# Rotary angles between projections, and modulation loads ahead of most of x, in a two-block transformer kernel

## What is computed

```python
mod = jax.nn.silu(c) @ w_ada[l] + b_ada[l]
shift1, scale1, gate1, shift2, scale2, gate2 = jnp.split(mod, N_MOD, axis=-1)
h = modulate(rmsnorm(x, norm1_w[l]), shift1, scale1)
proj = h @ w_in[l]
r_q, r_k, r_v, r_g, d_q, d_k, d_v, d_z, d_a, d_b = jnp.split(proj, cuts, axis=-1)
rq = rotary(heads(r_q, RET_HEADS), positions)
rk = rotary(heads(r_k, RET_HEADS), positions)
ret = retention(rq, rk, heads(r_v, RET_HEADS))
...
def rotary(x, positions):
    ang = positions.astype(jnp.float32)[..., None] * inv_freq
    cos, sin = jnp.cos(ang)[:, :, None, :], jnp.sin(ang)[:, :, None, :]
```

## Time and profile before

| | |
|---|---|
| median of 3 runs | 3334.73 us (3334.26 to 3335.98) |
| the profiled execution | 3336.45 us |
| its span | 3334.6 us |
| TensorE busy | 3054.4 us (92%), 11914 matmuls |
| VectorE, ScalarE, GpSimd busy | 929.2, 622.1, 477.9 us |
| first TensorE instruction | 43.79 us |
| first projection | 57.69 us |
| mean granted clock of TensorE | 0.961 |

### The profile page before, as it was taken

One profiled execution on the slowest core, in us unless ns is written; L12 is line 12 of the kernel. 1 busy time (PEld: TensorE's weight loads), 2 busy tenths in 40 slices (PEclk: granted clock), 3 DMA queues, 4 the chain that ended last, 5 costly groups with the idle time before them and its releaser, 6 DMA issues.

```text
span 3334.6 us, 30020 instructions
## 1 busy us (share of the span) xinstructions
PE 3054.4 (92%) x11914; PEld 1712.6 (51%) x11914; DVE 929.2 (28%) x1756; ACT 622.1 (19%) x1341; POOL 477.9 (14%) x473
## 2 busy tenths in 40 slices
PE   4998979788893999999959999999999999999999
PEld 2444534488642666666624455567444444444444
DVE  4322524466414111111133134587110000000101
ACT  2100222222120221111222211166210000000000
POOL 2002224354221000000021000066000000000000
PEclk9998989899996999999979999999999999999999
DMA  6442943100213999999761100030111111222222
GB/s 232 139 124 28 286 88 34 35 1 26 89 70 139 423 426 425 427 426 426 292 238 59 51 1 25 2 98 34 69 50 39 38 38 38 107 79 78 95 76 76
DMA packets 196510, 452.33 MB, mean 136 GB/s; under 512 B 27456, under 2 KB 125184, under 8 KB 183936
## 3 DMA queue, kind: packets, MB, share of 16 engines
q1 hardware_dynamic: 175409, 400.00, 34.3%
q10 hardware_dynamic: 14752, 27.66, 2.2%
q0 software_dynamic: 6192, 22.55, 1.7%
HBM read 413.21 MB, written 64.06 MB: 143 GB/s over the span
## 4 chain that ended last, share of the span: by engine, by line
PE 64%; DVE 2%; issue 1%; DMA 1%; ACT 1%; POOL 0%; POOLq 0%; ACTq 0%; SPq 0%; DVEq 0%
PE bank L3050 13%; PE bank L3081 13%; PE bank L1925 8%; PE bank L1928 7%; PE bank L2344 5%; PE bank L2923 3%; PE bank L2514 3%; PE bank L2512 2%; PE bank L2846 2%; PE bank L2856 2%; PE bank L232 1%; PE bank L1894 1%; PE bank L2727 1%; PE bank L2724 1%; PE bank L882 0%
## 5 line engine op out<-in xcount | busy, mean ns | idle before, releaser
L3081 PE MATMUL bank<-w_ff,uT 128*128 128x512 f32 x1024 | 441.9, 594 | 3.6 <-DVE hT L3138 3.6
L3050 PE MATMUL bank<-hT,w_ff 128*128 128x512 f32 x1024 | 439.8, 592 | 0.0
L3081 PEld LDWEIGHTS bank<-w_ff,uT 128*128 128x128 f32 x1024 | 195.0, 191 | 250.3 <-issue 244.2
L3050 PEld LDWEIGHTS bank<-hT,w_ff 128*128 128x128 f32 x1024 | 194.4, 190 | 243.9 <-issue 243.9
L489 PE MATMUL bank<-w_in,hT 128*128 128x512 f32 x512 | 224.6, 599 | 6.6 <-DMA w_in<-in_w_in 6.6
L1925 PE MATMUL bank<-e_w,e_xsT 128*128 128x256 f32 x832 | 187.2, 387 | 4.9 <-ACTq L2047 3.4
L1928 PE MATMUL bank<-e_w,e_xsT 128*64 128x256 f32 x1408 | 160.7, 388 | 29.7 <-issue 29.7
L1925 PEld LDWEIGHTS bank<-e_w,e_xsT 128*128 128x128 f32 x832 | 160.0, 194 | 36.4 <-issue 14.4
L2344 PE MATMUL bank<-w_gla,nT 128*128 128x512 f32 x384 | 168.8, 600 | 1.3 <-ACT nT L2308 1.3
L792 PE MATMUL bank<-hT,w_qkv 128*128 128x512 f32 x384 | 169.5, 600 | 0.0
L489 PEld LDWEIGHTS bank<-w_in,hT 128*128 128x128 f32 x512 | 97.9, 193 | 128.4 <-issue 126.4
(11 more groups left out here) (472 smaller groups left out, 3990.1 us busy)
## 6 DMA issues: line engine op xcount, KB each, us to landing
e_w<-in_w SPq DMA_DIRECT2D x117, 2048.0 KB, 28.8
w_ff<-in_w_ff SPq DMA_DIRECT2D x96, 512.0 KB, 3.3
wa<-in_w_ada SPq DMA_DIRECT2D x24, 1024.0 KB, 7.0
y_rows<-zero SPq DMA_DIRECT2D x1, 24064.0 KB, 120.8
y_rows<-e_y ACTq DMA_DIRECT2D x24, 512.0 KB, 8.7
w_in<-in_w_in SPq DMA_DIRECT2D x4, 2048.0 KB, 15.4
w_qkv<-in_w_in SPq DMA_DIRECT2D x12, 512.0 KB, 8.0
w_gla<-in_w_in SPq DMA_DIRECT2D x3, 2048.0 KB, 13.0
```

Source lines behind the costliest of these rows:

```text
L3050: t = pe.matmul(k.bank[2 * (j % 2) + h][:, :], w[:, f, :], hT[:, f, h * BANK:(h + 1) * BANK], start=f == 0, stop=f == NK - 1)
L3081: t = pe.matmul(k.bank[2 * n + h][:, :], b.uT[:, f, m * P:(m + 1) * P], b.ring[j % SLOTS][:, h * BANK:(h + 1) * BANK], start=f == 0, stop= ...
```

## The change

It has four parts. The load order on SyncE's queue is another: x's first load, then wa 3 to 7, then w_in's first quarter, then x's other three. Zeroing and bias of mod_acc are each split, into the first third and the rest; the rest's bias is loaded behind x. `rotary_vector` is split in two halves, called in the second quarter of the projections, ahead of the copies of products 3 and 5. ScalarE's two sines follow, ahead of the copies of products 4 and 6. No operation is dropped; there is one more memset and one more load of a bias.

```diff
+def front_x_load(k, s, b, n):
+
+    rows = k.io["x"][2 * n * P:2 * (n + 1) * P, :].rearrange("(m p) c -> p m c", p=P)
+    k.nc.sync.dma_start(b.x[:, 2 * n:2 * (n + 1), :], rows).then_inc(*(s.x_got_0, s.x_got_1, s.x_got_2, s.x_got_3)[n].up().inc)
...
@@ front_sync
     for q in range(RING):
         front_ada_load(k, s, b, q)
     sy.wait_ge(*s.acc_zero(1))
-    sy.dma_start(b.acc[0:1, :], io["b_ada"]).then_inc(*s.ada_bias.up().inc)
-    for n, got in enumerate((s.x_got_0, s.x_got_1, s.x_got_2, s.x_got_3)):
-        rows = io["x"][2 * n * P:2 * (n + 1) * P, :].rearrange("(m p) c -> p m c", p=P)
-        sy.dma_start(b.x[:, 2 * n:2 * (n + 1), :], rows).then_inc(*got.up().inc)
-        front_ada_load(k, s, b, RING + n)
-    front_ada_load(k, s, b, 7)
+    sy.dma_start(b.acc[0:1, 0:2 * D], io["b_ada"][:, 0:2 * D]).then_inc(*s.ada_bias.up().inc)
+    front_x_load(k, s, b, 0)
+    for q in range(RING, NK):
+        front_ada_load(k, s, b, q)
     front_w_load(k, s, b, 0)
+    for n in range(1, 4):
+        front_x_load(k, s, b, n)
+    sy.wait_ge(*s.acc_zero(2))
+    sy.dma_start(b.acc[0:1, 2 * D:], io["b_ada"][:, 2 * D:]).then_inc(*s.ada_bias.up().inc)
@@ front_gpsimd
-    g.memset(b.acc[:, :], 0.0).then_inc(*s.acc_zero.up().inc)
+    g.memset(b.acc[:, 0:2 * D], 0.0).then_inc(*s.acc_zero.up().inc)
+    g.memset(b.acc[:, 2 * D:], 0.0).then_inc(*s.acc_zero.up().inc)
@@ front_vector
-    rotary_vector(k, s, b)
     v.wait_ge(*s.acc_zero(1))
...
     for i in range(2):
         front_turned_vector(k, s, hT, affine, i)
+    v.wait_ge(*s.acc_zero(2))
+    v.wait_ge(*s.ada_bias(2))
     q = NK
     for at in range(4):
         for m in range(NT):
+            if at == 1 and m in (2, 4):
+                rotary_vector(k, s, b, m // 2 - 1)
@@ front_scalar
-    for n, out in enumerate((b.sin, b.cos)):
-        a.wait_ge(*s.angle_ready(n + 1))
-        a.activation(out[:, :, :], b.red[:, :, :], ACT.Sin).then_inc(*s.sine_made.up().inc)
...
+            if at == 1 and m in (3, 5):
+                n = m // 2 - 1
+                a.wait_ge(*s.angle_ready(n + 1))
+                a.activation((b.sin, b.cos)[n][:, :, :], b.red[:, :, :], ACT.Sin).then_inc(*s.sine_made.up().inc)
@@ rotary_vector
-def rotary_vector(k, s, b):
+def rotary_vector(k, s, b, n):
...
+    turn = (0.0, 0.25)[n]
+    if n == 0:
+        v.wait_ge(*s.pos_loaded(1))
+        v.tensor_copy(b.posf[:, :], b.pos[:, :]).then_inc(*V.up().inc)
         v.wait_ge(*V.now())
...
```

More of the change, by code:

```diff
@@ L523, in rotary_vector @@
     ang, cnt, red = b.ang[:, :, :], b.cnt[:, :, :], b.red[:, :, :]
-    v.wait_ge(*s.pos_loaded(1))
-    v.tensor_copy(b.posf[:, :], b.pos[:, :]).then_inc(*V.up().inc)
-    v.wait_ge(*V.now())
-    v.tensor_tensor(ang, wide(b.posf[:, :], 2, DH // 2), wide(k.c("inv_freq"), 1, NT), ALU.mult).then_inc(*V.up().inc)
-    for n, turn in enumerate((0.0, 0.25)):
-        v.wait_ge(*V.now())
[L530 to L543, removed]
+    turn = (0.0, 0.25)[n]
+    if n == 0:
+        v.wait_ge(*s.pos_loaded(1))
+        v.tensor_copy(b.posf[:, :], b.pos[:, :]).then_inc(*V.up().inc)
+        v.wait_ge(*V.now())
+        v.tensor_tensor(ang, wide(b.posf[:, :], 2, DH // 2), wide(k.c("inv_freq"), 1, NT), ALU.mult).then_inc(*V.up().inc)
+    v.wait_ge(*V.now())
+    v.tensor_scalar(cnt, ang, 1.0 / two_pi, turn, ALU.mult, ALU.add).then_inc(*V.up().inc)
+    v.wait_ge(*V.now())
+    v.tensor_scalar(cnt, cnt, magic, -magic, ALU.add, ALU.add).then_inc(*V.up().inc)
+    if n:
+        v.wait_ge(*s.sine_made(n))
+    src = ang
+    for part in parts:
+        v.wait_ge(*V.now())
+        v.scalar_tensor_tensor(red, cnt, -float(part), src, ALU.mult, ALU.add).then_inc(*V.up().inc)
+        src = red
+    v.wait_ge(*V.now())
+    v.tensor_scalar(red, red, turn * two_pi, np.pi, ALU.add, ALU.min).then_inc(*V.up().inc)
+    v.wait_ge(*V.now())
+    v.tensor_scalar(red, red, -np.pi, None, ALU.max).then_inc(*s.angle_ready.up().inc)
 Retention = namedtuple("Retention", "qk qkT t1 kw sT o ss state")
```

## The result

The changed kernel takes 3343.65 us (median of 6 runs) against 3334.49 before: a ratio of 1.0029, 95% interval 1.0019 to 1.0039. Later, with 8 runs against 13 of before, it took 3346.67 against 3334.15, ratio 1.0041 (1.0025 to 1.0057). It is slower by 9 to 14 us, as forecast; the forecast was 3345.2.

The account below looks back on a forecast made before the run. The first projection's start bounds the front; late x moves it from 57.7 to 68.2, +10.5 us, with clock and angles at 0. Added to 3336.45 that is 3347.0, less 1.7 for the median: 3345.2 us, range 3339.0 to 3347.8.

Parts of the forecast that it names:

- The mechanism: Front stage: x behind w_in holds ScalarE's squares, xn, transposes and columns; first projection at 68.2 instead of 57.7, +10.5 us.
- w_in's term: SyncE's load queue: w_in lands 12.5 us behind wa 7, the last x 19.9 us behind it, at 54.6.
- Rival (a): SyncE's queue: w_in is cheap, 5 us instead of 12.5; first projection at 60.7, +3.0 us, 3337.7; chance 0.12.
- The first link: VectorE's start: without the angles the first modulation step begins at 17.6, wa 7 lands at 34.7, eighth step ends at 37.1.
- the choice against 12.4: First modulation step: bias served in turn gives 17.6 and +10.5 us; bias slipping by gives 12.4 and +8.2 us.
- The columns' term: Chain from the last x through transposes, columns and hT to the first projection: 13.6 us without the modulation wait.
- the clock: TensorE's clock in the first projections: taken as 0, bounds 3.1 us gained or as much lost.
- Now w_in is the later by 3.4 us: Kernel before, first projection: w_in lands at 57.6, while the chain from x would allow a start at about 54.2.
- Cost nothing: Second quarter: angles and sines fit idle VectorE and ScalarE time; up to 11.7 us if that cover were gone.
- The split: VectorE's start: memset of a third ends at about 8.4, ahead of SyncE's third wa issue at 8.9, costing nothing.
- (b): SyncE's queue: x is served past w_in, last x at 42.2; not slower, -1.9 us, 3332.8; chance 0.05.
- (c): Front stage: modulation stays the last wait, needing its eighth step after 61.6 against 37.1 worked out; chance 0.01.

Follow-up runs that it names:

- e1: Kernel before with only the change's load order, angles in front and sum unsplit: 3350.85 us against 3332.98, ratio 1.0045.
- e3: Changed kernel with ScalarE doing squares, xn and hT of tiles 0 and 1 before the other tiles: 3326.13 us against 3332.98 before, ratio 0.9976.
- e4: Changed kernel with w_in's first load moved behind x's other three loads: 3333.95 us against 3332.98 before, ratio 0.9999.
- e7: Changed kernel with xn of tiles 0 and 1 early and the first bias load behind wa 0: 3324.89 us against 3332.59 before, ratio 0.9967.
- e6: Kernel before with ScalarE doing xn of tiles 0 and 1 early, loads and angles unchanged: 3333.24 us against 3332.59, ratio 0.9998.
- e8: Changed kernel with the angles and both sines back in front of the modulation steps: 3346.47 us against 3332.59 before, ratio 1.0038.
- e2: Changed kernel with the loads in the old order, angles moved and sum split: 3332.35 us against 3332.98 before, ratio 0.9992.

## Why the prediction was right, and where its sizes were off

**The mechanism was right.** x behind w_in, xn of tile 0 behind all squares, transposes and columns behind xn: e1, e3 and e4 each move one link and the first projection follows. The forecast of 68.2 for it met 68.22 by luck, since three errors cancel: wa 7 landed 1.7 us later than forecast (36.4, not 34.7), tile 6's square started 15.7 us behind that and not 19.9 (-4.2), and the first projection 16.1 us behind the square and not 13.6 (+2.5).

**w_in's term was too large.** "w_in and three 1 MB loads behind it need 19.9 us" was read from one execution, with 12.5 for w_in. It measured 8.0 in the changed kernel and 9.3 in the kernel before's second profile. So x's last load was in at 52.0, not 54.6, and tile 6's square followed the others at 52.1 with no wait for it. Rival (a), which wanted 5 us, was half true, and its result of +3.0 was not: w_in was 4.5 us faster and not 7.5, and the other two errors took 4.2 back.

**The first link was 0.2 off, the wa loads 1.7.** The first step came at 17.82 (17.6 forecast), released by the bias. Issued behind wa 0 alone (e7) the bias released it at 13.19, behind wa 0 to 2 (e3) at 17.65: the bias is served in turn, and the choice against 12.4 was right. The Trainium skill (DMA: Bandwidth & Descriptors, Queues, rings and completion order) states that each DMA engine consumes descriptors in ring order; the trace agrees, by the same two times. wa 7 was issued 0.5 us later than forecast and took 6.1 us, not the 4.9 of the earlier trace rows; the eighth step ended at 38.8, not 37.1.

**The columns' term was too small.** "13.6 from the last x" holds 4.63 us of columns. In the changed kernel they took 6.8. That is 2.2 of the 2.5 us; the other 0.3 is that the first projection waits for VectorE's half of hT and not for ScalarE's (1.70 us behind VectorE's first hT at 52.80 is 54.5 in the earlier trace rows, not 54.2). The instructions show why the columns took longer (weight loads of the columns, changed kernel, then before):

```profile
L480 PEld LDWEIGHTS bank<-consts,mod_acc x32: 333/333/337, 58.9 to 65.5; 128*128 128x128 f32 x32
```

```profile
L467 PEld LDWEIGHTS bank<-consts,mod_acc x32: 186/192/333, 47.6 to 51.8; 128*128 128x128 f32 x32
```

(nanoseconds: least, median, most.) The windows of the kernel before within its own columns (TensorE's matmuls, granted clock behind the count) and the weight loads of about the same stretches (mean in ns behind the comma):

```profile
47.60:50.40 2.80, 2.80 (x25) 0.97 0.88 99
51.00:52.20 1.20, 1.20 (x6) 0.50 0.79 222
```

```profile
L467 PEld LDWEIGHTS bank<-consts,mod_acc 128*128 128x128 f32 x25 | 3.0, 200 | 0.6 <-DVE mod_acc L342 0.6
```

```profile
L467 PEld LDWEIGHTS bank<-consts,mod_acc 128*128 128x128 f32 x6 | 1.4, 333 | 0.0
```

At 0.97 a load takes 200 ns, at 0.50 (1.2 GHz) 333. In the changed kernel all 32 take 333 to 337, and yet its windows give 1.00 there:

```profile
58.00:60.00 2.00, 2.00 (x12) 2.00 (x11) 0.00 (x0) 1.44 (x2) 0.00 (x0) 1.00 0.10 41
```

They give 1.00 for every stretch up to 250 us, and the first lower one (0.97) only behind that. That the engine ran at 1.2 GHz in the columns is inferred from the durations, against this figure. The columns ran slow throughout in e1 to e4, e6, e7 and both profiles of the changed kernel (6.8 to 7.0 us), and mostly fast in both of before and in e8 (3.95 to 4.63). I put the clock at 0 with bounds of 3.1 either way: 2.2 were lost in the columns and 1.4 came back in the first sixteen projections (8.80 instead of 10.17). That the same columns, behind the same transposes, fell on either side in e1 and e8 speaks against the change as its cause, though both profiles of before were fast and both of the changed kernel slow; what sets it was not found.

**The baseline was less firm than it looked.** "Now w_in is the later by 3.4 us" was 0.7 in the second profile of the kernel before, and the first projection 2.9 us earlier. From there to the changed kernel's it is 12.7 to 13.4 us, but 2.9 of them are the columns. At the columns' start, ahead of both w_in and the columns' speed, the changed kernel is 10.5 to 11.5 us later (58.39 and 59.10 against 47.86 and 47.58). That is what the late x costs there; how much of it reaches the projections depends on w_in's and the columns' pace in each execution. The medians, 9.2 and 12.5 us apart, lie on either side of the forecast.

**Cost nothing was right for the angles' new place** (idle time was used, no new wait), and taking them out of VectorE's start is worth about 3 us (e8 against the changed kernel in x's second load, 49.75 and 47.12; e2 against before). **The split** was costed at nothing and is (e1 and e8).

**Rivals (b) and (c)** did not occur: x was served behind w_in, and the eighth step ended 20 us before the columns began (38.8 and 59.1).

**Still open** is why w_in took 12.5 us behind wa 7 in one execution. It came once in ten profiles with that order, and no experiment was aimed at it. Open too is what sets the columns' pace.

## What to carry to other kernels

Loads that are moved ahead buy nothing until the engine that consumes the others stops waiting for them in its own program: here the loads' order (13 us lost alone) and ScalarE's order (nothing alone) together, with the angles' new place, gained 7 to 11 us. When two chains meet within a few us, the distance between them in a single profile can be that execution's accident, and the wait that the profile names needn't be the last one: compare it with the same wait elsewhere. A second profile of the kernel before is worth more than a finer reading of the first. A small load that a long chain waits for should be issued ahead of the large ones on its queue, but look next at what then bounds the chain: here 4.5 us earlier at the start became 0.3 at the end.

## What the runs showed of the hardware

The same 2 MB load, 2 KB a row, took 12.5 us behind the landing of the load ahead of it in one execution and 9.3 in another of the same kernel, and 7.3 and 8.0 in two of the changed one. A load of 1 MB needs about 2.5.

SyncE's issue of three x loads took 5.18 us in the changed kernel (31.18 to 36.36), where one issue on a queue with little in it takes 0.44. It ends as wa 7 lands (36.4), with w_in and all three x loads, 5 MB, then outstanding. In the six profiles with this order the three issues take 4.6 to 5.5 us and end within 0.5 us of wa 7's landing; in e4, where they stand ahead of w_in, they take 1.72. So the issuing engine itself is held, and what it issues next comes later. What sets the limit wasn't looked for.

In two kernels that reach the columns through the same instructions (e1 and e8) TensorE took 6.82 and 4.05 us for them. A difference of under 3 us between two single profiles at a place like this says nothing about a change.
